# Opening of a fused two-block transformer kernel: x turned unscaled, wider splits, first slab in halves, sine moved

## The reference, cut to what matters

```python
def rms_norm(x, g):
    y = x32 * lax.rsqrt(jnp.mean(x32 * x32, axis=-1, keepdims=True) + EPS)
    return (y * g).astype(x.dtype)
...
for i in range(DEPTH):                      # first block, two layers
    h = rms_norm(x, g[0])
    m = neighborhood_attention(...) if i % 2 == 0 else diff_attention(...)
    x = x + rms_norm(m, g[1])
    f = conv_glu_ffn(rms_norm(x, g[2]), ...)
    x = x + rms_norm(f, g[3])
    gate = sigmoid(rms_norm(x, g[4]) @ ple_w_gate[i])
    x = x + gate * (p[i] @ ple_w_proj[i])
...
# second block: swiglu, a mixer (linear attention beside latent attention with
# rotary sine and cosine of the positions), swiglu, a gated projection, a last rms_norm
```

## Time and profile before

| what | before |
|---|---|
| runs, median (lowest to highest) | 1225.48 us (1225.05 to 1225.56) |
| span of the profiled execution | 1226.3 us |
| PE busy | 1210.3 us, 99% of the span |
| PE weight loads busy | 1054.3 us, 86% |
| DVE busy | 945.3 us, 77% |
| ACT busy | 672.6 us, 55% |
| POOL busy | 138.0 us, 11% |
| HBM read and written | 212.30 MB and 1.06 MB, 174 GB/s over the span |

### The profile page before, as it was taken

The page is one execution under the profiler, slowest core; times in us unless marked ns, Lnnn a source line. Parts: engine busy times, 40 slices in busy tenths (PEclk is TensorE's granted clock), DMA queues, the critical chain, the costliest instruction groups (busy, mean ns, idle before and its releaser), DMA issues.

```text
span 1226.3 us, 17906 instructions
## 1 busy us (share of the span) xinstructions
PE 1210.3 (99%) x6995; PEld 1054.3 (86%) x6995; DVE 945.3 (77%) x1270; ACT 672.6 (55%) x1064; POOL 138.0 (11%) x257
## 2 busy tenths in 40 slices
PE   8999999999999999999999999999999999999997
PEld 7899888888879988888888988888896888888886
DVE  6757699888876588998888898776775778667665
ACT  6656644444575777444446845444675555443435
POOL 4000330000120012000002100000208420000002
PEclk9999999999999999999999999999999999999999
DMA  8834376565445445665554576555455136665540
GB/s 265 245 126 153 105 248 212 185 206 194 151 155 172 138 149 178 213 205 177 178 198 160 188 229 198 187 181 178 146 172 172 36 114 222 206 199 180 199 144 35
DMA packets 149015, 214.52 MB, mean 175 GB/s; under 512 B 4410, under 2 KB 114428, under 8 KB 148932
## 3 DMA queue, kind: packets, MB, share of 16 engines
q1 hardware_dynamic: 145596, 205.39, 51.0%
q0 software_dynamic: 1632, 4.71, 1.5%
q10 hardware_dynamic: 1704, 3.28, 0.8%
HBM read 212.30 MB, written 1.06 MB: 174 GB/s over the span
## 4 chain that ended last, share of the span: by engine, by line
PE 90%; DVE 5%; ACT 2%; DMA 1%; issue 1%; POOL 0%; POOLq 0%; ACTq 0%; DVEq 0%
PE work L2347 24%; PE work L2350 12%; PE acc L1946 10%; PE acc L1947 10%; PE acc L1948 10%; PE work L1946 5%; PE work L1947 5%; PE work L1948 5%; DVE w_lo L1261 2%; PE work L2156 2%; PE work L1968 2%; PE acc L2132 1%; PE work L2336 1%; PE work L2324 1%; PE work L2338 1%; PE work L2461 1%
## 5 line engine op out<-in xcount | busy, mean ns | idle before, releaser
L1261 DVE TENSOR_TENSOR w_lo<-raw,w_hi 128x2048 fp32r<-128x2048 f32 (+1 forms) x194 | 440.4, 2277 | 47.9 <-ACT w_hi L693 47.9
L693 ACT ACTIVATE w_hi<-raw 128x2048 fp32r<-128x2048 f32 (+2 forms) x193 | 365.2, 1899 | 69.3 <-PE work L2350 59.2
L2347 PE MATMUL work<-hT_both,w_hi 128*128 128x512 f32 x1280 | 318.8, 391 | 0.0
L2347 PEld LDWEIGHTS work<-hT_both,w_hi 128*128 128x128 f32 x1280 | 234.8, 188 | 45.1
L2350 PEld LDWEIGHTS work<-hT_both,w_lo 128*128 128x128 f32 x1280 | 174.6, 190 | 12.5
L2350 PE MATMUL work<-hT_both,w_lo 128*128 128x256 f32 x1280 | 178.5, 282 | 0.0
L1946 PE MATMUL acc<-w_hi,aux_hi 128*128 128x512 f32 x400 | 157.9, 395 | 0.0
L1947 PE MATMUL acc<-w_lo,aux_hi 128*128 128x512 f32 x400 | 156.7, 392 | 0.0
L1948 PE MATMUL acc<-w_hi,aux_lo 128*128 128x512 f32 x400 | 155.8, 390 | 0.0
L1048 ACT ACTIVATE aux_hi<-Z 128x256 fp32r<-128x256 f32 x88 | 36.9, 419 | 195.1 <-DVE Z L1671 107.1
L1642 DVE TENSOR_REDUCE Z<-work 128x256 f32<-128x512 f32 x88 | 60.6, 689 | 89.6 <-PE work L2350 87.8
(11 more groups left out here) (262 smaller groups left out, 1815.4 us busy)
## 6 DMA issues: line engine op xcount, KB each, us to landing
raw<-in_ffn_w_in SPq DMA_DIRECT2D x44, 1024.0 KB, 5.1
raw<-in_ffn_w_out SPq DMA_DIRECT2D x22, 1024.0 KB, 5.1
raw<-in_w_gate SPq DMA_DIRECT2D x22, 1024.0 KB, 5.4
raw<-in_w_up SPq DMA_DIRECT2D x22, 1024.0 KB, 5.3
raw<-in_w_down SPq DMA_DIRECT2D x22, 1024.0 KB, 5.0
raw<-in_na_w_qkv SPq DMA_DIRECT2D x12, 1024.0 KB, 7.5
raw<-in_da_w_qkv SPq DMA_DIRECT2D x12, 1024.0 KB, 5.1
raw<-in_ple_w_gate SPq DMA_DIRECT2D x8, 1024.0 KB, 5.1
```

The lines of the kernel that those rows point to most:

```text
L693: act.activation(w_hi[:, n % RING, 0:size], raw[:, n % RAW, 0:size], ACT.Copy).then_inc(hi_done, 1)
L1261: dve.tensor_tensor(w_lo[:, n % RING, 0:size], raw[:, n % RAW, 0:size], w_hi[:, n % RING, 0:size].bitcast(F32), ALU.subtract).then_inc(lo_ ...
L2347: pe.matmul(b.rearrange("p (e s) -> p e s", e=2), v[0][:, k, cols(c % 2)], hT_both[:, k, :, :], start=k == 0, stop=False)
```

## The change

It changes seven things. Stage 0 joins UNSCALED, while SCALED_OUT names the stages (1 and 4) in which the factor also goes on the output. Both row tiles of x are turned at once, raw, into blocks of 256 columns (`turn_first`), and each is split by one ACT and one DVE instruction. Slab 0 is loaded and converted in two halves. The squares and `powers` come after the splits; `turn_scales(0)` lays the factors out as a row, ACT copies it (`rb0`), and DVE multiplies it on all 16 column blocks (`column_scaled`), which ACT copied before; the value rows get theirs in ACT's copy. `first_columns` now handles slab 0 and slab 1 in the same way, and the first value rows come ahead of the taps and of the first scores. The sine goes to the second attention, lambda's exponential behind the first unit's exponentials, and `lambdas` and `rotary` into DVE's list of the first attention. The DMAs of lambda, positions and table go from ACT's queue to POOL's, `load_rpb(0)` no longer waits for `hi_done` 2, the gains' DMA goes behind `weights_turned(0, 3)`, and fewer dummy matmuls are issued (2, 4 and 6 instead of 10, 5, 8 and 2).

```diff
-UNSCALED = [1, 4, 6, 7, 8]
+UNSCALED = [0, 1, 4, 6, 7, 8]
+SCALED_OUT = [1, 4]
...
+        def first_block(k):
+            return acc[:, k % 4, k // 4 * S:(k // 4 + 1) * S]
...
+                if n == 0:
+                    sp.dma_start(dst[:, 0:4, :], src[:, 0:4, :]).then_inc(first_half, 16)
+                    sp.dma_start(dst[:, 4:8, :], src[:, 4:8, :]).then_inc(landed[0], 16)
...
-            powers("pre0.1")
-            pool.wait_ge(landed[0], 16)
-            pool.tensor_copy(w_hi[:, 0, :], raw[:, 0, :]).then_inc(hi_done, 1)
...
+            pool.wait_ge(first_half, 16)
+            pool.tensor_copy(w_hi[:, 0, first], raw[:, 0, first]).then_inc(first_hi, 1)
+            pool.wait_ge(landed[0], 16)
+            pool.tensor_copy(w_hi[:, 0, second], raw[:, 0, second]).then_inc(hi_done, 1)
+            pool.dma_start(z(11864, 12120), bass.AP(w["da_lambda"].tensor, 0, [[0, P], [1, 256]])).then_inc(lam_loaded, 16)
+                pool.dma_start(posi[:, :], w["positions_2"][0].rearrange("(t p) -> p t", p=P)).then_inc(pos_loaded, 16)
+                pool.dma_start(tT[:, :], w["t5_table"].rearrange("b h -> h b")).then_inc(t5_loaded, 16)
             load_rpb(0)
+            powers("pre0.1")
...
             evacuated(act, G["vec"])
-            tile_parts(0, 0)
-            tile_parts(0, 1)
+            for k in range(KT):
+                if k < 4:
+                    act.wait_ge(turn_full, k + 1)
+                else:
+                    act.wait_ge(part_ready, k - 3)
+                split(hT_hi[:, k, :], first_block(k), gains_of(0, k))
+            pre(0, 0)
             act.wait_ge(hi_done, 1)
             fed[0] = 1
+            feed(2)
+            pre(0, 1)
             feed(3)
-            columns_out(0, 0)
-            columns_out(0, 1)
-            act.wait_ge(rot_ready, 1)
-            act.activation(trig[:, :, :, :].rearrange("p a b c -> p (a b c)"), rot, ACT.Sin).then_inc(trig_ready, 1)
-            act.wait_ge(lam_sum, 1)
-            act.activation(lame[:, :], lamc[:, 0:2], ACT.Exp).then_inc(lam_exp, 1)
+            scales_out(0)
...
+            def column_scaled(n):
+                g, f = G[f"c0.{n}"], n // 4 * 2 + n % 2
+                if n == 0:
+                    dve.wait_ge(scales_ready, UNSCALED.index(0) + 1)
+                full(dve, g)
+                src, roots = [v.rearrange("p (t c) -> p t c", t=T) for v in (bank(g)[:, 0:S], rb0)]
+                dst = (kT if n // 2 % 2 else qT)[:, f, :].rearrange("p (t c) -> p t c", t=T)
+                dve.tensor_tensor(dst if n // 2 % 2 else backwards(dst), src, roots, ALU.mult)\
+                    .then_inc(bank_free[g % WORK], 1)
...
             def attention0():
                 feed(b + 3)
+                for n in range(4):
+                    column_scaled(n)
                 expand(0)
+                lambdas()
+                feed(b + 4)
                 scores(0, 0)
+                taps_out()
                 expand(1)
-                taps_out()
-                feed(b + 4)
                 scores(0, 1)
+                rotary()
                 expand(2)
                 feed(b + 5)
                 expand(3)
...
                 feed(b + 6)
+                column_scaled(4)
                 feed(b + 7)
                 output(0)
+                feed(b + 8)
+                column_scaled(5)
                 output(1)
-                feed(b + 8)
                 feed(b + 9)
+                column_scaled(6)
+                column_scaled(7)
                 scores(0, 2)
...
+            def turn_first():
+                for t in range(T):
+                    pe.wait_ge(x_loaded[t], 16)
+                    for i in range(4):
+                        for k in (i, i + 4):
+                            ins = pe.transpose(first_block(k)[:, cols(t)], x[:, t, cols(k)], ident[:, :])
+                        if t == 1:
+                            ins.then_inc(turn_full, 1)
...
             def attention0():
-                first_columns()
-                half_columns(0, 2)
-                half_columns(0, 3)
+                first_columns(0)
+                first_columns(1)
+                value_rows(0, 0, 0, 0)
+                turn_taps()
                 unit_scores(0, 0)
-                turn_taps()
-                value_rows(0, 0, 0, 0)
+                value_rows(0, 0, 0, 1)
                 unit_scores(0, 1)
```

More of the change, by code:

```diff
@@ L458, in split_order @@
         def split_order(ph):
-            return list(range(KT)) if PHASES[ph] == "ple" else BLOCKS
+            return list(range(KT)) if PHASES[ph] == "ple" or ph == 0 else BLOCKS
         FIRST_UP = [(k, i) for ks in (BLOCKS[:4], BLOCKS[4:]) for i in range(2) for k in ks]
+        def first_block(k):
+            return acc[:, k % 4, k // 4 * S:(k // 4 + 1) * S]
         def turned_block(ph, t, step):
@@ L591, in _ @@
             ins.then_inc(freq_ready, 1)
-            pool.wait_ge(hi_done, 2)
+            first, second = slice(0, SLAB // 2), slice(SLAB // 2, SLAB)
+            pool.wait_ge(first_half, 16)
[3 more added lines that the diff above has]
+            pool.dma_start(z(11864, 12120), bass.AP(w["da_lambda"].tensor, 0, [[0, P], [1, 256]])).then_inc(lam_loaded, 16)
+            with nc.allow_non_contiguous_dma(reason="256 positions and 256 table entries, once"):
+                pool.dma_start(posi[:, :], w["positions_2"][0].rearrange("(t p) -> p t", p=P)).then_inc(pos_loaded, 16)
+                pool.dma_start(tT[:, :], w["t5_table"].rearrange("b h -> h b")).then_inc(t5_loaded, 16)
             load_rpb(0)
+            powers("pre0.1")
             link(pool.memset(wmask[:, :], 0.0))
@@ L893, in values_out @@
             def values_out(ph, half, t):
-                g = G[f"v{ph}.{half}.{t}"]
-                evac(g, vtok[:, t, half * 512:(half + 1) * 512], bank(g))
+                g, dst = G[f"v{ph}.{half}.{t}"], vtok[:, t, half * 512:(half + 1) * 512]
+                if ph == 0:
+                    i, c = E[f"pre0.{t}"]
+                    full(act, g)
+                    act.wait_ge(rstd_done, i + 1)
+                    act.activation(dst, bank(g), ACT.Copy, scale=rstd[:, c:c + 1]).then_inc(bank_free[g % WORK], 1)
+                else:
+                    evac(g, dst, bank(g))
             def attention0():
                 b = B[0]
-                columns_out(0, 2)
-                columns_out(0, 3)
                 feed(b + 4)
                 unit_exps(0, 0)
+                act.wait_ge(lam_sum, 1)
+                act.activation(lame[:, :], lamc[:, 0:2], ACT.Exp).then_inc(lam_exp, 1)
                 feed(b + 5)
@@ L960, in attention3 @@
                 feed(b + 7)
+                angles = trig[:, :, :, :].rearrange("p a b c -> p (a b c)")
+                act.activation(angles, angles, ACT.Sin).then_inc(trig_ready, 1)
                 unit_exps(3, 0)
@@ L1896, in rotary @@
                 link(dve.tensor_scalar(rot[:, 64:128], rot[:, 64:128], math.pi / 2, None, ALU.add))
-                dve.tensor_scalar(rot, rot, 3.1415925, -3.1415925, ALU.min, ALU.max).then_inc(rot_ready, 1)
-            tile_parts(0, 0, range(4))
-            normed(0, 1)
-            tile_parts(0, 0, range(4, 8))
-            tile_parts(0, 1)
+                dve.tensor_scalar(trig[:, :, :, :].rearrange("p a b c -> p (a b c)"), rot, 3.1415925, -3.1415925,
+                                  ALU.min, ALU.max).then_inc(rot_ready, 1)
+            for k in range(KT):
+                split(hT_lo[:, k, :], first_block(k), hT_hi[:, k, :], k + 1, gains_of(0, k))
+            first, second = slices(SLAB // 2)
+            dve.wait_ge(first_hi, 1)
+            dve.tensor_tensor(w_lo[:, 0, first], raw[:, 0, first], w_hi[:, 0, first].bitcast(F32), ALU.subtract)
+            dve.wait_ge(hi_done, 1)
+            dve.tensor_tensor(w_lo[:, 0, second], raw[:, 0, second], w_hi[:, 0, second].bitcast(F32), ALU.subtract)\
+                .then_inc(lo_done, 1)
+            fed[0] = 1
             feed(2)
-            lambdas()
-            rotary()
             def taps_out():
-                dve.wait_ge(lam_exp, 1)
-                link(dve.tensor_tensor(lamc[:, 2:3], lame[:, 1:2], lame[:, 0:1], ALU.subtract))
-                dve.tensor_scalar(lamc[:, 3:4], lamc[:, 2:3], LAMBDA_INIT, None, ALU.subtract)
                 g = G["taps"]
```

94 lines of the change are left out of this document (46 added, 48 removed).

## The result

| | before | after |
|---|---|---|
| median of 9 runs (lowest to highest) | 1225.52 us (1225.05 to 1226.85) | 1228.81 us (1227.67 to 1229.92) |
| ratio to before, 95% interval | | 1.0027 (1.0018 to 1.0035) |
| span of the profiled execution | 1226.3 us, in a second profile 1223.2 | 1225.9 us, in a second profile 1225.8 |
| PE busy | 1210.3 us, second 1208.6 | 1206.6 us |

The change makes the kernel 0.27% slower, 3.3 us. The spans say the opposite at first sight, and that was the fault of the first profile of before: where a profiled execution's own time is known, it is 1.8 us above its span (1225.01 and 1223.2 for the second profile of before, 1227.67 and 1225.9 for the changed kernel), so the first profile of before, 1226.3, was of an execution some 2.6 us slower than the median. Some 2.1 us lie in the mixer, where PE's granted clock was 0.60 from 940 to 944 us.

A forecast was written before the change was run, and what follows sets the result against it. PE was taken as the bound, its opening a chain through DVE and ACT. Opening -4.3, c3 wait -0.5, factors +0.25, slab 4 +3.2, c6 +2.1 make +0.75 on 1225.48: 1226.3 us, range 1223.2 to 1228.5.

The forecast's parts named there:

- Opening, lo products at 14.4: Opening: PE's lo products on slab 0 start at 14.4 instead of 18.66 us, 4.3 us gained.
- First scores at 26.2: First attention on PE: first scores start at 26.2 instead of 27.32 us, with value rows and taps ahead of them.
- PE ready for slab 4 at 37.7: Ahead of slab 4: without another wait PE would reach it at 37.7 instead of 42.26 us.
- a drain: Opening's table load: rival with the skill's 1.38 us drain exposed as well, 1227.6 us; chance 0.03.
- Slab 3, the step that failed: Slab 3's transfer: with the table it follows slab 2, lands at 22.4, hi part from 23.5, lo part done at 27.6.
- lands as late after its issue as before, or 1 us beyond: Transfers rival: slab 3 or table late, DVE's queue, second table and slab 8 move 0.8 to 1.8 us; 1227.4; chance 0.14.
- just this of slab 8: Slab 8's transfer: the table keeps most of the DMA engine until through, so the slab's end stays despite earlier issue.
- The factors, put at nothing: Factors in the opening: squares and powers behind the splits, due at turn_scales about 18 us, done by 17; no cost.
- DVE's queue ahead of slab 4: DVE, first scores to slab 4's lo part: 13.35 us from 27.5, ending at 40.9; PE waits 3.2 us.
- the low clock only for the opening: Opening, clock rival: PE stays at 1.2 GHz beyond 15 us, scores full 2.5 us later; +3.2, 1228.7; chance 0.08.
- c6 behind slab 8: Third unit's scores: c6, copied behind slab 8's lo part, is ready at 58.9; PE waits 2.1 us, scores at 59.0.
- The sum: Up to the third unit's scores: all terms together make +0.75 us, taken as the same difference on the median.

The follow-up runs named there:

- k14: k8 with column_scaled(4) ahead of slab 5's lo part on DVE; 1222.29 us, 0.9977 of before.
- k10: Changed kernel with the first bias table issued by ACT behind feed(3) and slab 3's lo part ahead of expand(0) on DVE; 1228.29 us, 1.0023 of before.
- k6: Changed kernel with 17 dummy matmuls ahead of half_columns(0, 4) and c6's copy ahead of slab 8's lo part on DVE; 1226.29 us, 1.0006 of before.
- k5: Changed kernel with 17 dummy matmuls on PE ahead of half_columns(0, 4); 1229.53 us, 1.0029 of before.
- k13: Changed kernel with dummy matmuls 4 and 3 instead of 2 and 4 in the opening; 1229.40 us, 1.0032 of before.
- k4: Changed kernel with rotary cut in two and moved into DVE's idle times before the scores; 1225.60 us, 1.0004 of before.
- k9: k8 with the bias table issued later by ACT, slab 3's lo part ahead of expand(0), rotary's second half behind scores(0, 1); 1225.13 us, 0.9995 of before.
- k7: k4 with c6's copy, slab 4's lo part and values_out(0, 0, 0) put earlier; 1223.53 us, 0.9985 of before.
- k8: k7 with the function table's load early in ACT's idle time and dummy matmuls 4 and 3 for 2 and 4; 1223.41 us, 0.9981 of before.
- k1: Changed kernel with 34 dummy matmuls on PE ahead of half_columns(0, 4); 1232.47 us, 1.0061 of before.

## Why the prediction was wrong, point by point

- **Opening, lo products at 14.4:** 14.24, right, with the table load exposed (6.80, 1.28 us). First scores at 26.2: 25.91. PE ready for slab 4 at 37.7: its last value product starts at 37.30 and ends at 37.69. The Trainium skill, "ScalarE: Activation LUTs", What ACT_TABLE_LOAD costs, adds a drain to the load; the next ACTIVATE at 8.10 leaves no room for one here either.
- **Slab 3, the step that failed:** "the same 7.8 us of transfers can follow slab 2", landed at 22.4, hi part from 23.5. It began at 24.99, and DVE's scores at 29.14 instead of 27.5, 1.6 us late. I had the rows of the slower case, 9.8 us from issue to hi part, counted them to the landing, took a value 2 us below, and left the slower case to a rival ("lands as late after its issue as before, or 1 us beyond", 1227.4). It was that rival, at its far end: 10.8. My working let the transfers follow slab 2 in whatever order; but the table, issued 2 us ahead of slab 3, had 89% of the DMA engines' time from 16 to 20 us. The prediction had said just this of slab 8 (the table keeps the engines until it is through) and did not apply it to slab 3. Nor did an earlier issue help: over the thirteen profiles with the table on POOL's queue slab 3 was issued between 12.73 and 15.04, and its hi part began between 24.99 and 27.11, in no order with the issue (12.73 and 26.24 in k14, 14.21 and 24.99 in the changed kernel). With the table behind it, it began at 21.26 (k10). The least transfer time of any slab, 5.1 us, is from beyond the first 60 us, where none took less than 5.9.
- **The factors, put at nothing:** `powers` was to be done by 17; `rstd` was ready at 20.59, since two one-column operations took 2.2 us each beside DVE's lo parts. Here it cost PE 0.3 us, and more in every shorter opening.
- **DVE's queue ahead of slab 4:** 13.35 us predicted, 13.0 measured (29.14 to 42.14). Its end 42.14 instead of 40.9, PE's wait 4.5 instead of 3.2.
- **The clock behind that wait, missed:** I weighed the low clock only for the opening. Behind the wait of 4.5 us the first 20 matmuls came 0.21 us apart (1.2 GHz), which made c4 2.0 us longer (4.96 against 2.97 with the clock held up in k6). The Trainium skill, "TensorE: Matmul & The Clock Gate", Part 1, says that the array returns to the lower clock when it has been idle; the trace agrees, with 0.53 from 42 to 47 us. That was against this change, and belonged to every wait that I priced.
- **c6 behind slab 8:** a wait of 2.1 us up to 59.0 predicted. c6 was copied at 60.05, later by DVE's 1.2 us; PE came then too, slowed by its clock, so the trace shows no wait. With the clock held up it shows one of 2.0 us (k5). Right, and hidden. Slab 8, issued at 45.5 instead of 47.2, was converted from 55.48 instead of 54.47, as the table's second half was issued at 43.31 instead of 42.23: an earlier issue of the slab gained nothing, as said.
- **The sum:** +0.75 predicted at the third scores, +2.03 measured against the earlier trace rows. The 1.28 between them is what slab 3's lateness made of slab 4 (42.20 instead of 40.9), handed down by DVE; the clock's 2.0 us took the place of c6's 2.1. That the two were of one size is luck: the sum held one delay of about 2 us where the runs show two side by side. No run gives the 1.28 back by itself: in k10, with slab 3 early, the table and then c6 took its place. (1225.48 + 0.75 is 1226.2; the prediction wrote 1226.3.)
- **From there to the median:** +3.3 us. I compared with a profiled execution that was itself 2.6 us slow, 0.5 of it in its opening: against the second profile of before the scores are 2.5 us late and the span 2.7. The remaining 0.6 would fit the changed kernel's opening, whose turns hang on when the clock rises (k13); both profiles of before have their turns behind the rise, 8 in 1.04 to 1.09 us. That it is this is not shown.

## What to carry to other kernels

Before an opening is shortened, find the last thing that its successor waits for: here DVE's first scores waited for the table before and for slab 3 after, both from one full DMA, at 29 us either way. Work put into another engine's list belongs into that list's idle time, not to where it is first needed. And price a wait of PE with the slow matmuls behind it; two delays that end together must be taken away together.

## What the runs showed of the hardware

- PE's clock fell behind waits of 4.0 to 4.9 us ahead of slab 4 (every profile that has one) and of 2.0 us (k4 and k9: c4 in 4.44 and 4.47 us), not behind 0.8 to 0.9 us (k6, k7, k8, k14). Behind the same wait of 1.13 us at 360 us it fell in k7 and k8 and in no other profile, and behind 1.24 us at 939 us in the first profile of before, but not behind 1.38 and 1.60 us at 941 to 947 in k1.
- In the opening the pace of 128-column records went from 0.21 or 0.22 us to 0.12 at another moment in each execution, so 16 turns took 1.94 us (k14) to 3.62 (k1), from starts at 4.80 to 5.34. The profile's granted clock says 1.00 all through the first 8 us, so there the level can only be read from the pace.
- A one-column operation of POOL took 2.2 us while DVE made a lo part, and 0.22 to 0.28 without one. POOL of the changed kernel:

```profile
17.36 2.20 POOL L571 TENSOR_SCALAR ms<-ssq 128x1 f32<-128x1 f32 x1
19.66 0.28 POOL L571 TENSOR_SCALAR ms<-ssq,ms 128x1 f32<-128x1 f32 x1
```

  DVE's lo part of slab 2 was at 17.19 to 19.48. This is a new wait of the change, as `powers` now stands beside lo parts: PE waits for `rstd` 0.3 us in the changed kernel and 1.6 in k14. The Trainium skill, "SBUF — State Buffer", Who interferes with whom, has a lock that a DVE operation with two inputs in SBUF and a GpSimd operation that reads SBUF take in turn; the rows agree.
- The bias table took 11.4 us from its first issue to DVE's use from POOL's queue (12.23 to 23.62 in k8) and 12.2 and 12.9 from ACT's (15.32 to 27.50 in k10, 15.55 to 28.50 in k9). For the slab beside it the difference was large: in 16 to 20 us POOL's queue, in packets of 3.5 KB on average, had 89% of the engines' time, and ACT's, in packets of 0.9 KB, 22.5% (k10).
